# Stick-breaking heads: suffix sums over key tiles added up on the vector engine, then one matmul per triangle

## The reference, cut to what matters

```python
z = q . k * scale
mask = (s[None, :] < t[:, None]) & valid[None, :end]
log_beta = jax.nn.log_sigmoid(z)
log_1m = jnp.where(mask, log_beta - z, 0.0)          # minus softplus(z)
rev = lax.cumsum(log_1m, axis=3, reverse=True)
suffix = jnp.concatenate([rev[..., 1:], jnp.zeros_like(rev[..., :1])], axis=-1)
w = jnp.where(mask, jnp.exp(log_beta + suffix), 0.0)
o = w @ v
```

## Time and profile before

| what | value |
|---|---|
| median of 3 runs | 1152.04 us (1151.4 to 1154.93) |
| the profiled execution's own time | 1150.38 us |
| its span in the trace | 1148.5 us |
| mean granted TensorE clock | 0.981 of full |
| PE busy | 1061.6 us, 92% |
| DVE busy | 668.8 us, 58% |
| ACT busy | 475.1 us, 41% |
| POOL busy | 243.4 us, 21% |

### The profile page before, as it was taken

The page is one execution under the profiler, slowest core; times in us unless marked ns, Lnnn a source line. Parts: engine busy times, 40 slices in busy tenths (PEclk is TensorE's granted clock), DMA queues, the critical chain, the costliest instruction groups (busy, mean ns, idle before and its releaser), DMA issues.

```text
span 1148.5 us, 16700 instructions
## 1 busy us (share of the span) xinstructions
PE 1061.6 (92%) x6437; PEld 919.4 (80%) x6437; DVE 668.8 (58%) x1084; ACT 475.1 (41%) x842; POOL 243.4 (21%) x159
## 2 busy tenths in 40 slices
PE   5999899899899899999989999999997888999996
PEld 5997677798898677798878778889876776888896
DVE  4768778917757778937325665757456875123213
ACT  4344444424334344524247656622454553222221
POOL 1214000002205000003130302123422333243232
PEclk9999999999899899999999999999998999999998
DMA  7323001233233001133230202113211011232321
GB/s 251 101 93 110 19 20 37 75 111 95 71 106 109 21 19 37 38 110 80 81 108 1 74 1 74 38 38 105 79 55 38 1 38 54 75 99 85 116 69 74
DMA packets 79778, 80.51 MB, mean 70 GB/s; under 512 B 5440, under 2 KB 77248, under 8 KB 79696
## 3 DMA queue, kind: packets, MB, share of 16 engines
q1 hardware_dynamic: 78080, 77.04, 21.3%
q10 hardware_dynamic: 1616, 2.36, 0.6%
HBM read 77.30 MB, written 2.10 MB: 69 GB/s over the span
## 4 chain that ended last, share of the span: by engine, by line
issue 40%; PE 40%; DVE 7%; POOL 6%; ACT 4%; DMA 1%; POOLq 0%; SPq 0%; DVEq 0%; ACTq 0%
PE ps L1503 12%; PE ps L1504 11%; PE ps L1505 11%; PE ps L1760 2%; ACT pw L893 2%; DVE pwt L1262 2%; POOL small L458 1%; DMA raw<-in_w_in 1%; DVE small L1440 1%; PE ps L1763 1%; POOL t L468 1%; POOL sq L468 1%; DVE sp L1325 1%; POOL small L447 1%; PE ps L1748 1%
## 5 line engine op out<-in xcount | busy, mean ns | idle before, releaser
L486 POOL TENSOR_TENSOR wlo<-raw,whi 128x2048 fp32r<-128x2048 f32 (+1 forms) x31 | 135.9, 4386 | 351.7 <-ACT whi L726 351.7
L1503 PE MATMUL ps<-whi,hhi 128*128 128x256 f32 x544 | 158.3, 291 | 15.6 <-DVE wlo L973 8.3
L1504 PE MATMUL ps<-wlo,hhi 128*128 128x256 f32 x544 | 156.4, 288 | 0.0
L1505 PE MATMUL ps<-whi,hlo 128*128 128x256 f32 x544 | 156.4, 288 | 0.0
L1503 PEld LDWEIGHTS ps<-whi,hhi 128*128 128x128 f32 x544 | 107.1, 197 | 17.9 <-DVE wlo L973 9.1
L1503 PE MATMUL ps<-hhi,whi 128*128 128x512 f32 x288 | 115.1, 400 | 2.5 <-ACT tg L908 1.7
L1504 PE MATMUL ps<-hlo,whi 128*128 128x512 f32 x288 | 114.0, 396 | 0.0
L1505 PE MATMUL ps<-hhi,wlo 128*128 128x512 f32 x288 | 113.7, 395 | 0.0
L1504 PEld LDWEIGHTS ps<-wlo,hhi 128*128 128x128 f32 x544 | 107.0, 197 | 0.0
L1505 PEld LDWEIGHTS ps<-whi,hlo 128*128 128x128 f32 x544 | 107.0, 197 | 0.0
L726 ACT ACTIVATE whi<-raw 128x2048 fp32r<-128x2048 f32 (+1 forms) x35 | 63.4, 1814 | 101.9 <-PE ps L1505 101.8
(11 more groups left out here) (289 smaller groups left out, 2637.2 us busy)
## 6 DMA issues: line engine op xcount, KB each, us to landing
raw<-in_w_in SPq DMA_DIRECT2D x45, 1024.0 KB, 5.3
raw<-in_w_out SPq DMA_DIRECT2D x12, 1024.0 KB, 5.0
raw<-in_w_branch_swa SPq DMA_DIRECT2D x4, 1024.0 KB, 5.0
raw<-in_w_in SPq DMA_DIRECT2D x4, 512.0 KB, 3.9
raw<-in_w_branch_sb SPq DMA_DIRECT2D x4, 512.0 KB, 3.5
out<-x SPq DMA_DIRECT2D x4, 512.0 KB, 2.6
x<-in_x ACTq DMA_DIRECT2D x3, 512.0 KB, 6.8
ws<-in_spatial_w SPq DMA_DIRECT2D x2, 512.0 KB, 7.6
```

Source lines behind the costliest of these rows:

```text
L486: pool.tensor_tensor(wlo[s][:, 0:n, :], raw[s][:, 0:n, :], whi[s][:, 0:n, :].bitcast(F32), ALU.subtract).then_inc(slab_split, 1)
L1503: pe.matmul(out_ap, lhsT=lhi(k), rhs=rhi(k), start=first and k == 0, stop=False, skip_group_check=True)
L1504: pe.matmul(out_ap, lhsT=lhi(k), rhs=rlo(k), start=False, stop=False, skip_group_check=True)
L1505: m = pe.matmul(out_ap, lhsT=llo(k), rhs=rhi(k), start=False, stop=last and k == n - 1, skip_group_check=True)
```

## The change

DVE adds the terms over the key tiles before they are rounded: tile 2 gets tile 3 added on the queries that both have, then tile 1 gets tile 2, then tile 0 gets tile 1. After that, tile j holds the sum over its own and all later tiles. The sum of all keys from a given one is then the triangle over tile j (row >= column) plus the other triangle (row < column, the new constant `comp`) over tile j + 1, so each target tile has at most two matmuls, and the meta bank has one over tile 0 in place of four. The three additions each wait for the one before (`sp_summed`), and the first waits for both 640-column pieces (`sp_made`). `sp_done` is raised for the meta piece as before, and for the other two pieces only once all additions are done. The table of constants is laid out anew, with the same size: `mask_sb` and the first half of `mask_sw` now share one tile, and `comp` takes the room.

```diff
-        mask_sb, mask_sw, mask_sw0 = consts_r[:, 384:512], consts_r[:, 512:768], consts_r[:, 768:912]
+        mask_sb, mask_sw, mask_sw0 = consts_r[:, 384:512], consts_r[:, 384:640], consts_r[:, 640:784]
+        comp = consts_r[:, 784:912]
...
+        sp_made, sp_summed = sem("sp_made"), sem("sp_summed")
...
                 for n in range(3):
                     v = piece_of(sp_[:, h % 2, :], n)
                     dve.wait_ge(ln_done, 3 * h + n + 1)
-                    dve.scalar_tensor_tensor(v, scores(h, n), 0.0, v, ALU.max, ALU.add).then_inc(sp_done, 1)
+                    m = dve.scalar_tensor_tensor(v, scores(h, n), 0.0, v, ALU.max, ALU.add)
+                    if n == 0:
+                        m.then_inc(sp_done, 1)
+                    else:
+                        m.then_inc(sp_made, 1)
+                dve.wait_ge(sp_made, 2 * h + 2)
+                v = sp_[:, h % 2, :]
+                for n, j in enumerate((2, 1, 0)):
+                    own, next_ = Z_AT[j] + P, Z_AT[j + 1]
+                    w = Z_WIDTH[j + 1]
+                    dve.tensor_tensor(v[:, own:own + w], v[:, own:own + w], v[:, next_:next_ + w], ALU.add)\
+                       .then_inc(sp_summed, 1)
+                    dve.wait_ge(sp_summed, 3 * h + n + 1)
+                dve.sem_inc(sp_done, 2)
...
                     for to in range(NT):
-                        for j in range(NT - 1, to - 1, -1):
-                            pe.matmul(z_cols(h, to, j), lhsT=tri if to == j else ones_, rhs=terms(j), start=False,
-                                      stop=part == 1 and j == to, skip_group_check=True)
-                    for j in range(NT):
-                        pe.matmul(meta_z(h)[:, P * j:], lhsT=ones_[:, 0:META], rhs=terms(j), start=False, stop=False,
+                        if to < NT - 1:
+                            pe.matmul(z_cols(h, to, to + 1), lhsT=comp, rhs=terms(to + 1), start=False, stop=False,
+                                      skip_group_check=True)
+                        pe.matmul(z_cols(h, to, to), lhsT=tri, rhs=terms(to), start=False, stop=part == 1,
                                   skip_group_check=True)
+                    pe.matmul(meta_z(h), lhsT=ones_[:, 0:META], rhs=terms(0), start=False, stop=False,
+                              skip_group_check=True)
```

More of the change, by code:

```diff
@@ L1988, in constant_tiles @@
     own = masked(c <= r)
-    tiles = [np.where(r >= c, -1.0, 0.0), np.full((P, P), -1.0), np.eye(P), masked(r < c),
-             masked(c > r), own, masked(r < P - META + c[:, 0:META]), own]
+    tiles = [np.where(r >= c, -1.0, 0.0), np.full((P, P), -1.0), np.eye(P), masked(c > r), own, masked(r < P - META + c[:, 0:META]), own,
+             np.where(r < c, -1.0, 0.0)]
     return np.concatenate(tiles, 1).astype(np.float32)
```

## The result

The changed kernel takes **1169.72 us** (median of 4, 1168.91 to 1170.45) against 1152.46 for the kernel before on the same chip (median of 4): ratio 1.0139, 95% interval 1.0118 to 1.0161. It is 17.3 us slower by the medians, and 13 us above the upper end of the range. The profiled execution spans 1168.7 us at a mean granted clock of 0.964, against 1148.5 us at 0.981.

A forecast was written before the change was run, and what follows sets the result against it. PE and the loop ACT, DVE, PE were taken to bound in turn: four heads' gain (5.6) given back by four lateness terms (about 7) less 1.4 of slack, +0.27 us; 1152.3 us by median, range 1148.3 to 1156.7.

The forecast's parts named there:

- rival 3: TensorE's clock falls as its idle time before the sums grows: +3.6 us, 1155.9; chance 0.20 together with Rival 4.
- The saving of a head's sums: PE's matmuls for a head's sums, with fewer columns, take 1.40 us less a head, 11.2 for all eight.
- The additions: Three added DVE instructions of 128, 256 and 384 columns a head, with hand-overs: 1.33 us.
- The lateness of the terms: DVE's low parts of the terms end 1.60 us late in a head, behind ACT's delayed roundings.
- that of ACT's roundings: ACT's two large roundings start only after the additions and end 1.90 us late.
- The gaps: PE's idle time before the sums of heads 2, 4, 6 and 7: 2.8, 1.9, 1.9 and 2.7 us.
- The wait before the scores: PE newly waits for `sb_read` before the scores of heads 3 and 5, 1.3 us each.
- The sum: All shifts followed round the loop to head 7 and carried to the end: +0.27 us, 1150.65 for the profiled execution.
- The range: Whole kernel's time from 1148.3 to 1156.7 us, from bounds on the additions' price and the saving; outside under 2 in 10.
- Rival 2: The copy of wr at head 1 slips between POOL's two subtractions, head 2's terms 2.8 us earlier: 1149.5; chance 0.10.
- Rival 4: A DVE addition falling into a POOL subtraction waits up to 4.6 us: 1156.9; part of the 0.20 with rival 3.

The follow-up runs named there:

- e3: The whole change plus forty unread 512-column matmuls before the values of heads 1, 3, 5 and 6: 1154.85 us, ratio 1.0031 to the kernel before.
- e2: The new products with the old softplus and without the additions, against the kernel before (a price, no version): 1144.0 us, ratio 0.9925.
- e4: The change at heads 0, 1, 3 and 5 alone, other heads as in the kernel before: 1151.8 us, ratio 0.9996.
- e5: The changed kernel with columns 640 to 1280 first, each piece handed to ScalarE once added up: 1159.08 us, ratio 1.0034 to the kernel before.
- e6: e5 with only two of the three additions at heads 2, 4, 6 and 7: 1150.93 us, ratio 0.9983 to the kernel before.
- e8: The changed kernel with e3's unread matmuls at heads 1 and 3 alone: 1159.44 us, ratio 1.0066 to the kernel before.
- e1: The additions as in the change, but the products of the kernel before, so no column taken from TensorE: 1165.47 us, ratio 1.0115.
- e7: The change at heads 2, 4, 6 and 7 alone, other heads as in the kernel before: 1167.73 us, ratio 1.0123.
- e10: e5 with unread matmuls filling the gaps at heads 1, 3, 5 and 6: 1149.72 us, ratio 0.9978 to the kernel before.
- e12: The kernel before with six unread matmuls in its own two gaps at head 1: 1152.17 us, ratio 1.0001.

## Why the prediction was wrong

It was wrong in one step, the price of half clock in rival 3: the sum has no term for it, and the rival that has one prices a fall at 1.8 us, where the two long ones took 8.5 us each. It also left out one wait of PE. The steps that could be read from rows came out.

- *The saving of a head's sums* was put at 1.40 us. At full clock the sums of head 0 run from 613.00 to 616.38, 3.38 us; in the kernel before they ran from 611.19 to 615.97, 4.78. That is the 1.40 of the rows, not the 1.10 that the forecast estimated from the spacing in the Trainium skill, TensorE: Matmul & The Clock Gate, section Back-to-back issue gap.
- *The additions* were put at 1.33 us; they take 1.34. *The lateness of the terms* was put at 1.60; it is 3.81 - 2.06 = 1.75; that of ACT's roundings was put at 1.90, and is 2.01 (2.83 us from softplus to roundings at head 4, where it was 0.82). *The gaps* before the sums were put at 2.8, 1.9, 1.9, 2.7; they are 2.78, 1.83, 1.84, 2.85. *The wait before the scores* was put at 1.3; it is 1.29 and 1.28 in e3.
- *One wait was not listed*: 1.83 us before the values of head 1, 0.42 before. Its terms stand in the forecast, 2.80 early against 1.40. In all five traces in which it has no unread matmuls in it or behind it (the changed kernel, e2, e4, e5, e6) half clock follows within 7 us; in e3 and e8, with 12 unread matmuls right behind it, none does. In e1 and e7, where it is 0.42, the gap of 2.79 before the sums of head 2 has no fall behind it. It is a pattern of single traces, but the first long stretch may well need this wait too.
- *The sum* of +0.3 us is borne out as far as the runs reach, where the clock does not fall more than before: spans corrected for the two mean clocks are equal, with the reserve of some 4 us said above, and e3, which adds only fillers, is at +2 us by medians (0 to 7 by the interval of its ratio).
- *The range*: its upper end leaves out the 0.04 x 4 of the saving's own bound, 1156.9 with it. The measured time is far outside by either.
- *Rival 2*: the first copy of `wr` did slip in between POOL's subtractions (it took 1.21 us at 634.96), and the next one stood from 636.20 for 5.14 us, as argued against it. Nothing was gained.
- *Rival 4*: no addition was held; the three shapes agree with the straight line.
- **Rival 3 was mis-sized.** "Nine matmuls of 512 columns at half speed cost 9 x 0.2 = 1.8 us ... at least twice more than today: +3.6, 1155.9. Chance 0.20". The mechanism is the one that happened, with falls behind three of the four gaps before sums; the price of one was taken from a fall in the kernel before, which lay on matmuls of 512 columns and was over in 3.4 us. Behind the gaps at heads 2 and 4 lie the thinned sums, the scores and the 24 matmuls of 16 columns. At half clock the sums of head 4 take 5.5 us in place of 3.4 and the 24 matmuls 5.0 in place of 2.6; the clock is down through all of them, 17.1 us, and PE loses half of that, 8.5 us, for each. The third fall, at head 7, lasts 6.8 us. The chance was also too low: the forecast itself listed six new gaps of 1.3 to 2.8 us in 110 us, beside a row in which a wait of 3.0 us was followed by a fall.

What was shown: that nearly all of the loss is half clock (e3, and the ten runs of e5); that PE's idle gaps bring it (e1 without any lost column, e3, e8, e10 with gaps closed); that the gaps and the thinned sums cost more together (17.3) than one by one (3.9). That the sparse work behind a gap, few columns in each matmul, is what stretches a fall from 3.4 to 17 us was read from traces and not isolated: no run took the 16-column matmuls away. e1 against e7 at head 4 supports the part of the thinned sums, and so does e2, whose thin sums have no gap of over 0.6 us before them and no stretch over 6.8 us. Against it stands the end of e1, where the sums of head 7 are not thinned and the half clock lasts 10.2 us, longer than the changed kernel's 6.8.

## What to carry to other kernels

Where PE's busy share is high but a loop through the other engines is equally long, taking work off PE and putting about as much on the loop (here 1.40 us off a head, terms 1.75 us later) gives nothing back in time and turns into idle gaps. Price such a gap by the work that stands behind it, and not by a fall that lay elsewhere: here one gap of 1.83 us was followed by a fall that cost 8.5 us, through sums, scores and 16-column matmuls, and ended 3.2 us after matmuls of 512 columns had begun. List every wait of PE that the shifts imply, also those not at the changed step. If the gap cannot be closed, matmuls of 512 columns that nobody reads, placed inside it, held the clock here (15 us of 17 back in e3); six of them in the kernel before cost nothing that could be measured (e12).

## What had not been expected of the hardware

- The same program runs from 1148.7 to 1162.8 us (e5), in steps that follow the mean clock. The kernel before went from 1149.9 to 1156.6 over all its runs, and its mean clock tells less: at 0.981 alone it took 1149.9 to 1154.0.
- A gap of 1.83 us was followed by 17 us of half clock at head 4 and one of 1.84 us by none at head 6, in the same trace.
- Forty added matmuls made the changed kernel 1.3% faster.
- A copy on VectorE was admitted between two of GpSimd's back-to-back subtractions, and the copy right behind it was held for the whole next one (5.14 us in place of 0.83).
